# A feed-forward product by sub-blocks: GpSimd's weight sums one turn later, and two low halves ahead of the first output sums

## The reference, cut to what matters

```python
m = rmsnorm(h, g_pre_ffn[l])
m = jnp.square(jax.nn.relu(m @ w_ffn_up[l])) @ w_ffn_down[l]     # 1024 -> 4096 -> 1024
h = h + rmsnorm(m, g_post_ffn[l])
return h[:, N_META:]
```

## Time and profile before

| what | value |
|---|---|
| median of 3 runs | 1560.98 us (1555.43 to 1563.23) |
| profiled execution | 1556.64 us, span 1554.9 us |
| TensorE matmul busy | 1464.2 us, 94% of the span |
| VectorE busy | 1051.2 us, 68% |
| ScalarE busy | 801.7 us, 52% |
| GpSimd busy | 295.8 us, 19% |
| mean DMA rate over the span | 166 GB/s |
| `store_quad`, issue to landing, median of 16 | 8.6 us |
| `load_quad`, issue to landing, median of 16 | 8.9 us |

### The profile page before, as it was taken

The page is one execution under the profiler, slowest core; times in us unless marked ns, Lnnn a source line. Parts: engine busy times, 40 slices in busy tenths (PEclk is TensorE's granted clock), DMA queues, the critical chain, the costliest instruction groups (busy, mean ns, idle before and its releaser), DMA issues.

```text
span 1554.9 us, 36731 instructions
## 1 busy us (share of the span) xinstructions
PE 1464.2 (94%) x15384; PEld 1245.8 (80%) x15384; DVE 1051.2 (68%) x1514; ACT 801.7 (52%) x1388; POOL 295.8 (19%) x307
## 2 busy tenths in 40 slices
PE   6999999995998999999969996999999999999998
PEld 6999999994777777777748875878888888888886
DVE  6244436444878888889766769998888655544555
ACT  6254445343877878778645543333333343433452
POOL 6233325340101011010100004543333000100000
PEclk9999999996999999999989998999999999999999
DMA  4433562646513214121054467797777585675553
GB/s 183 139 127 122 199 223 75 229 122 201 147 40 91 55 51 112 34 51 37 4 149 120 138 230 232 269 311 277 264 251 249 193 306 190 226 275 190 194 185 135
DMA packets 119132, 257.53 MB, mean 166 GB/s; under 512 B 9136, under 2 KB 49200, under 8 KB 118720
## 3 DMA queue, kind: packets, MB, share of 16 engines
q1 hardware_dynamic: 114448, 238.81, 46.7%
q10 hardware_dynamic: 3744, 13.85, 2.2%
q0 software_dynamic: 784, 2.65, 0.7%
HBM read 167.14 MB, written 86.85 MB: 163 GB/s over the span
## 4 chain that ended last, share of the span: by engine, by line
PE 44%; DVE 3%; ACT 1%; issue 1%; DMA 1%; SPq 0%; DVEq 0%; ACTq 0%
PE tail_bank L2653 20%; PE tail_bank L2583 18%; PE tail_bank L2568 5%; PE tail_bank L2531 1%; DVE tail_tl L2351 1%; DMA tail_w_rest<-in_w_out 1%; DVE tail_al L2285 0%; PE tail_bank L2576 0%; ACT mixed_wh L2100 0%; SPq L1806 0%; DVE tail_al_f L2303 0%; DVE tail_xf L2272 0%; DVE tail_tl_f L2346 0%; DVE tail_tl_f L2342 0%; DVE tail_al L2281 0%
## 5 line engine op out<-in xcount | busy, mean ns | idle before, releaser
L2376 DVE TENSOR_TENSOR tail_tl<-tail_down_raw,tail_th 128x1024 fp32r<-128x1024 f32 x84 | 102.0, 1256 | 95.7 <-ACT tail_th L2070 95.7
L2070 ACT ACTIVATE tail_th<-tail_down_raw 128x1024 fp32r<-128x1024 f32 x84 | 84.4, 1052 | 128.4 <-PE tail_bank L2653 113.6
L2653 PE MATMUL tail_bank<-tail_th 128*128 128x512 f32 x336 | 131.0, 390 | 0.0
L2653 PE MATMUL tail_bank<-tail_th,tail_tl 128*128 128x512 f32 x336 | 131.0, 390 | 0.0
L2653 PE MATMUL tail_bank<-tail_tl,tail_th 128*128 128x512 f32 x336 | 130.7, 389 | 0.0
L689 PE MATMUL inproj_acc<-xn_xl,inproj_wh 128*128 128x348 f32 (+1 forms) x384 | 123.4, 321 | 0.0
L689 PE MATMUL inproj_acc<-xn_xh,inproj_wl 128*128 128x348 f32 (+1 forms) x384 | 123.2, 321 | 0.0
L689 PE MATMUL inproj_acc<-xn_xh,inproj_wh 128*128 128x348 f32 (+1 forms) x384 | 123.2, 321 | 0.0
L569 DVE TENSOR_TENSOR inproj_wl<-xn_raw,inproj_wh 128x1024 fp32r<-128x1024 f32 x27 | 34.7, 1286 | 94.6 <-ACT inproj_wh L445 94.6
L2583 PE MATMUL tail_bank<-tail_th,tail_ah 128*128 128x512 f32 x240 | 93.7, 391 | 2.9 <-DVE tail_al L2285 1.2
L2583 PE MATMUL tail_bank<-all_mh,tail_ah 128*128 128x512 f32 x212 | 84.8, 400 | 10.6 <-DVE tail_al L2281 10.6
(11 more groups left out here) (380 smaller groups left out, 4413.1 us busy)
## 6 DMA issues: line engine op xcount, KB each, us to landing
tail_down_raw<-u_scratch SPq DMA_DIRECT2D x56, 512.0 KB, 3.6
tail_raw<-in_w_up SPq DMA_DIRECT2D x32, 512.0 KB, 6.7
tail_w_quad<-in_w_down SPq DMA_DIRECT2D x16, 1024.0 KB, 8.9
d_scratch<-tail_w_quad SPq DMA_DIRECT2D x16, 1024.0 KB, 8.6
u_scratch<-tail_u_sums SPq DMA_DIRECT2D x16, 1024.0 KB, 5.5
tail_down_raw<-d_scratch SPq DMA_DIRECT2D x32, 512.0 KB, 4.5
xn_raw<-in_w_in SPq DMA_DIRECT2D x27, 512.0 KB, 4.8
p_scratch<-inproj_out ACTq DMA_DIRECT2D x26, 520.0 KB, 2.7
```

The source lines that it names most:

```text
L2070: act.activation(op_high[b][:, j, :], down_raw[c % len(down_raw)][:, j, :], ACT.Copy).then_inc(down_high, 1)
L2376: dve.tensor_tensor(op_low[b][:, j, :], down_raw[c % len(down_raw)][:, j, :], op_high[b][:, j, :].bitcast(F32), ALU.subtract).then_inc(dow ...
L2653: last = pe.matmul(downs[pass_of(c) % 2][o][:, :], u[:, own_tile], w[:, f * HALF:(f + 1) * HALF], start=(n == 0 and f == 0 and j == 0), st ...
```

## The change

Both lists of quads get an empty entry in front, and `W_DURING` goes in pairs up to quad 5; and in turn 1 of VectorE's list `hidden_sums(0)` moves behind the low halves of A11 and A12 of pair 2. Loads of quads are issued one turn later each (quads 0 and 1 in turn 1 and not ahead of it, ... quad 15 in turn 13 and not 12). Stores of quads 0 to 4 are issued one turn later; those of 5 to 15 stay in their turns. So every quad is now loaded in one turn and stored in the next, where before that was so of quads 0 to 4 only, and from quad 6 on (loaded in turn 3, stored in turn 5) the store came two turns behind the load.

```diff
-W_BEFORE = [[0, 1], [2, 3], [4, 5]] + [[i] for i in range(6, 2 * DOWN_CHUNKS)]
-W_DURING = [[0, 1], [2, 3]] + [[i] for i in range(4, 2 * DOWN_CHUNKS)]
+W_BEFORE = [[], [0, 1], [2, 3], [4, 5]] + [[i] for i in range(6, 2 * DOWN_CHUNKS)]
+W_DURING = [[], [0, 1], [2, 3], [4, 5]] + [[i] for i in range(6, 2 * DOWN_CHUNKS)]
...
                 c11(q)
-                if q == 1:
-                    hidden_sums(0)
                 if q < LASTP:
                     of_raw(A11, q + 1, 0, 0)
                     of_raw(A12, q + 1, 0, 1)
+                if q == 1:
+                    hidden_sums(0)
                 if q > 1:
                     c21(q - 1)
                     hidden_sums(q - 1)
```

## The result

Timed side by side, the changed kernel takes 1580.44 us (median of 4 runs, 1577.60 to 1581.79) and the kernel before 1560.45 (1555.43 to 1563.23): 20.0 us slower, ratio 1.0131 [1.0109, 1.0153]. Forecast were 17.9 us more and 1579.0.

What follows compares the result with a forecast made beforehand. VectorE was taken to set the end up to the third pair, TensorE from turn 4. Terms 1.9 + 3.2 + 10.7 + 2.1 = 17.9 us slower: 1574.5 from the profiled execution, 1579 as median; range 1569 to 1591, widened to 1558 to 1591.

Steps and rivals of the forecast that it cites:

- The first stretch: Turns 1 and 2: `one(2)` starts at 953.0 instead of 963.19, T of turn 2 comes 12.3 us ahead.
- Rival C: Turn 1 on VectorE: late hidden sums 0 delay `c22(1)`, undoing the reorder; 2 to 3 us above before; chance 0.02.
- What was late next: SyncE's queue up to T of turn 6: pairs' rounds of 27.2 us lose the 12.3 us and 1.9 more.
- the closed loop: SyncE's queue: wait for GpSimd's quad, store it, outputs and sums, load the next; 27.2 us for pairs, 19.7 for singles.
- Single quads: Turns 6 to 14: a round of 19.7 us, 0.4 more than a turn, costs 3.2 us over eight turns.
- Turn 14: Down product's first chunk comes late: `five(14)` starts at T + 16.2, not 5.6, costing 10.7 us, plus 2.1 for the clock.
- A: Turn 2 onward: stores land early enough and the lead stays; 8 to 12.3 us faster, about 1550; chance 0.13.
- B: Single quads' loop runs under 19.3 us and catches up by turn 14; within 4 us of before, about 1560; chance 0.15.
- D: Loop takes 20.5 us a round and stalls each of turns 4 to 6; 32 us and more slower; chance 0.04.

Runs made afterwards that it cites:

- e3_store_behind: The changed kernel with the quad's store put behind the hidden sums' store in SyncE's queue; 1554.01 us against 1559.68 for the kernel before, ratio 0.9955.

## Why the prediction was right

**The first stretch** came as reckoned, the clock included. `one(2)` was put at 953.0, which with the 1.9 us that this execution was late is 954.9; it started at 955.34, and its wait is 0.3. That is 9.8 us ahead; the granted clock is 1.00 from 950 to 970, and T of turn 2 is 11.8 ahead of the 12.3 forecast. GpSimd's first quad was to start at 965.5 (967.4 with the shift) and started at 967.83. Rival C, the second edit undone by `c22(1)`, didn't happen: that lead at T of turn 2 has `four(1)` in it.

**What was late next** was named rightly, the closed loop, and in its right order. The pairs' round was to be 27.2 us and was 26.6 and 26.9 (GpSimd's first sums at 967.83, 994.44 and 1021.31). Hidden sums start 9.6 us behind the quad's store (1034.43 to 1044.06) and not 10.5: the store of the earlier trace rows was a little long. From these hidden sums to T of turn 6 were 12.6 us and not 13.2, and the last pair's store was 0.7 earlier than forecast. So T of turn 6 was 0.4 ahead and not 1.9 behind, 2.3 us on the good side.

**Single quads** were the term mis-sized. "I take 19.7, as the only row with one load" gave 3.2 us over eight turns; the round was (1232.05 - 1048.60) / 9 = 20.4, and T of turn 14 had lost 9.1 us since T of turn 6. GpSimd's share was right (6.6). The other part, 13.1 from that one row, is 13.8 as the mean of the nine waits of GpSimd for its load, which scatter from 12.6 to 15.0. The row of the first single quad, which ends the last pairs' round with 14.2, and that of the last:

```profile
1048.60 1.65 POOL L1964 TENSOR_TENSOR tail_w_quad<-tail_w_quad 128x512 f32<-128x512 f32 x1 [14.19 <-DMA tail_w_quad<-in_w_down]
...
1232.05 1.26 POOL L1964 TENSOR_TENSOR tail_w_quad<-tail_w_quad 128x512 f32<-128x512 f32 x1 [13.83 <-DMA tail_w_quad<-in_w_down]
```

The pairs' row of 13.9, which I had kept as the upper bound, was the typical one. A single row of a quantity that scatters by 2 us was taken to 0.4 us, in a place where the difference to the turn is multiplied by eight. That it lay within the bounds kept the range.

What the 13.8 are made of can be seen in part. The forecast counted the five transfers from the quad's store to the next load, 3.67 MB. But `c22`'s store and `load_w` are issued right behind the load and move their bytes while it is still under way. What is issued later lands later: from issue to landing the quad's store, first in its burst, takes 4.3 us, the sums' store 7.5 and the quad's load, last of the five, 10.3 (medians of 16). Over the nine rounds, from the store's issue to the load's landing, the core's DMA engines are busy for 91 to 96% and move 4.0 to 4.7 MB (mean 4.3) at 297 to 322 GB/s, and the two shortest of these times, 12.6 and 12.9 us, carry 4.0 and 4.2 MB where the two longest, 15.0 and 14.7, carry 4.7 each (windows):

```profile
1096.69:1109.25 12.56, 11.04 (x49) 8.77 (x48) 9.23 (x15) 3.39 (x6) 0.00 (x1) 1.00 0.93 317
1136.61:1151.56 14.95, 14.95 (x66) 11.95 (x65) 11.35 (x18) 3.92 (x7) 0.00 (x1) 1.00 0.95 315
```

**Turn 14** cost 14.5 us for the 12.8 forecast: 12.2 for the 10.7 up to `five(14)`, and 2.3 for the 2.1 of the clock (`five(14)` itself took 5.0 us, 2.7 before). The quad's store was issued at T + 17.2 (16.4), `low_of_chunk(0)` started at T + 21.5 (20.8) and `five(14)` at T + 17.7 (16.2): each 0.7 to 1.5 later. But the 16.4 is not what its own terms make: 19.7 + 19.3 - 13.2 - 10.5 = 15.3. If the landing of `load_down(0)` was reckoned from the same store, as it reads, the term would have been 9.6 and the sum 16.8. The measured 17.2 is two rounds, 39.8 us from the store at 1197.59 to that at 1237.37, less the 22.6 from the first of them to T. So the slip brought the forecast nearer, and that was luck.

**The sum.** -0.4 + 9.1 + 14.5 = 23.2 us in the stretch of the profiled executions, for 1.9 + 3.2 + 12.8 = 17.9: 2.3 less, 5.9 more and 1.7 more. The medians differ by 20.0 only, since the profiled execution of before lay 3.8 us under its median and that of after 1.4 above. So 1579.0 came as near as it did to 1580.4 in part by chance: the single-quad term was short by 5.9 us of the trace. The range was not a sum either: the ends of the terms as given add up to -1 and 33 us, not 8 and 30.

**The rivals.** A, the lead stays: no, T was 10.1 us ahead in turn 4 and 0.4 in turn 6. B, a loop under 19.3 that catches up: no in the changed kernel. The run with short sums shows that a loop without GpSimd's sums has room: 14.9 us in its closest round, and no stall. Its 381 GB/s was one stretch of ten us; over whole rounds it was at most 322. The estimate of 10.4 us for the five transfers, which the Trainium skill's formula gave in the prediction (DMA: Bandwidth & Descriptors, "Anatomy of one DMA"), isn't borne out by any round here: 12.6 to 15.0. That section gives the formula for DMAs issued on GpSimd's queue, and these are SyncE's. GpSimd's own accesses aren't what makes them long, since it stands idle while they run. D had the right stalls, 2.7, 4.8 and 1.7 us at T of turns 4 to 6, and a round near its 20.5, but those stalls are how the 12.3 us of lead are used up, not a cost beyond them; its 32 us took them as coming on top.

**Still open**: why the rate over a round stays near 310 GB/s with the DMA engines busy for 91 to 96%. Fewer bytes or another order among them (the load first) weren't tried, only the store's place in the queue was; so it isn't shown how much of a round a smaller or later `load_w` would save.

## What to carry to other kernels

When a step is moved in a queue that runs in order, write down the round that it closes (wait, what is queued behind it, load, work, wait again) and set it against the turn of the engine that bounds: under the turn it costs nothing, over it the excess comes in every turn and no lead lasts. The cure here needed neither fewer bytes nor less work, only the waiting store put behind the stores that others need: 26 us with the same instructions. When the length of the transfers in a round is reckoned, what is queued behind the one that is waited for counts too. A term that is multiplied by the number of turns needs the mean of several rows, not the one row that looks closest.

## What the runs showed of the hardware

**GpSimd and VectorE slow each other both ways.** In turn 14, where VectorE had 0.85 us of work in ten, the sums of GpSimd follow each other in 1.34 us; beside a busy VectorE it is 1.73 and 1.70 (1048.60, 1050.33, 1052.03 above). VectorE's own sum is 1.75 with GpSimd and 0.69 without, so each loses, and short sums gave 8.0 us back to a kernel whose GpSimd is busy for 19% of the span.

```profile
1232.05 1.26 POOL L1964 TENSOR_TENSOR tail_w_quad<-tail_w_quad 128x512 f32<-128x512 f32 x1 [13.83 <-DMA tail_w_quad<-in_w_down]
1233.39 1.26 POOL L1966 TENSOR_TENSOR tail_w_quad<-tail_w_quad 128x512 f32<-128x512 f32 x1
```

The Trainium skill (SBUF — State Buffer, "SBUF: two separate sides") has the pair of ports that both use as a lock held for a whole instruction, the other standing meanwhile. These rows agree with it: VectorE's delay is 1.1 us for an instruction of 512 columns and of 2048, near the length of one GpSimd sum, 1.26 here.

**An issue on SyncE's queue isn't of fixed length.** Behind an idle stretch the store of a quad takes 0.38 us to issue; right behind it the two outputs' stores take 1.56 together, the sums' store 1.24 and the next quad's load 1.33, so that load goes out 3.3 us behind the quad's store (timeline of SyncE, changed kernel):

```profile
1197.59 0.38 SPq L1869 DMA_DIRECT2D d_scratch<-tail_w_quad  x1
1198.01 1.56 SPq L1853 DMA_DIRECT2D u_scratch<-tail_c  x2
1199.61 1.24 SPq L1858 DMA_DIRECT2D u_scratch<-tail_u_sums  x1
1200.89 1.33 SPq L1864 DMA_DIRECT2D tail_w_quad<-in_w_down  x1
```

With the loop opened the outputs' stores have gone out before, one by one as VectorE makes them, and the three that are left in a row take 0.37, 0.51 and 1.13 (timeline of SyncE, `e3_store_behind`):

```profile
1151.77 0.37 SPq L1858 DMA_DIRECT2D u_scratch<-tail_u_sums  x1
1152.19 0.51 SPq L1869 DMA_DIRECT2D d_scratch<-tail_w_quad  x1
1152.74 1.13 SPq L1864 DMA_DIRECT2D tail_w_quad<-in_w_down  x1
```
